# A two-layer hybrid decoder trunk: the third projection tile of layer 1 by token halves, and the norm's sums in column strips

## What is computed

```python
for l in range(DEPTH):                       # 2
    m = _mixer(_rmsnorm(h, norm_mix_pre[l]), ..., w_in[l], ..., w_out[l])
    h = h + _rmsnorm(m, norm_mix_post[l])
    f = _swiglu(_rmsnorm(h, norm_ffn_pre[l]), w_gate_up[l], w_down[l])
    h = h + _rmsnorm(f, norm_ffn_post[l])
# _rmsnorm(x, w) = x * rsqrt(mean(x * x) + EPS) * w
```

## Time and profile before

| | |
|---|---|
| Median of 3 runs | 1385.88 us (1385.72 to 1387.19) |
| The profiled execution | 1384.18 us, span 1382.4 us |
| Granted TensorE clock | 0.998 of 2.4 GHz |
| PE busy | 1362.3 us (99%) |
| VectorE busy | 1039.6 us (75%) |
| ScalarE busy | 634.8 us (46%) |
| GpSimd busy | 100.5 us (7%) |

### The profile page before, as it was taken

How to read it: one execution, slowest core, us unless ns; L and a number is a source line. 1 busy time by engine, 2 the same in 40 slices (tenths; PEclk the granted TensorE clock), 3 DMA queues, 4 the chain that set the end, 5 groups by cost and what they waited for, 6 DMA issues and landing times.

```text
span 1382.4 us, 29088 instructions
## 1 busy us (share of the span) xinstructions
PE 1362.3 (99%) x12172; PEld 1339.7 (97%) x12172; DVE 1039.6 (75%) x1675; ACT 634.8 (46%) x1230; POOL 100.5 (7%) x141
## 2 busy tenths in 40 slices
PE   8999999999999999999999999999999999999997
PEld 8999999999999999999989999999999999999996
DVE  7746796768999898754586458968789989886545
ACT  5235554557545455422442364545575445454221
POOL 0001221000000000011000012110000000000110
PEclk9999999999999999999999999999999999999999
DMA  6332243122333333355413313321232333333552
GB/s 210 107 107 78 67 116 105 45 69 81 103 108 114 101 101 108 115 174 183 130 62 108 111 60 99 107 94 36 79 92 93 120 95 112 104 106 121 176 178 93
DMA packets 67491, 147.46 MB, mean 107 GB/s; under 512 B 20128, under 2 KB 23584, under 8 KB 67360
## 3 DMA queue, kind: packets, MB, share of 16 engines
q1 hardware_dynamic: 59536, 119.90, 27.3%
q0 software_dynamic: 7824, 25.70, 5.5%
HBM read 132.79 MB, written 12.78 MB: 105 GB/s over the span
## 4 chain that ended last, share of the span: by engine, by line
PE 88%; DVE 8%; ACT 1%; issue 1%; DMA 1%; SPq 0%; DVEq 0%; ACTq 0%
PE PS L676 48%; PE PS L1231 8%; PE PS L1232 8%; PE PS L1233 8%; PE PS L682 5%; DVE Wl L1875 1%; DVE hT L1913 1%; DVE Xl L1892 1%; DVE mT L1912 1%; PE PS L870 1%; DVE conv L2002 1%; PE PS L1197 1%; PE PS L1016 1%; PE PS L842 1%; PE PS L854 1%
## 5 line engine op out<-in xcount | busy, mean ns | idle before, releaser
L1310 ACT ACTIVATE Wh<-stage 128x1024 fp32r<-128x1024 f32 x143 | 151.1, 1058 | 327.6 <-PE PS L676 299.5
L676 PE MATMUL PS<-Xh,Wh 128*128 128x260 f32 x1376 | 285.5, 289 | 2.9 <-DVE Xl L1934 2.2
L676 PE MATMUL PS<-Xh,Wl 128*128 128x260 f32 x1376 | 277.0, 283 | 0.0
L676 PE MATMUL PS<-Xl,Wh 128*128 128x260 f32 x1376 | 276.5, 282 | 0.0
L1875 DVE TENSOR_TENSOR Wl<-stage,Wh 128x1024 fp32r<-128x1024 f32 x143 | 174.6, 1222 | 105.7 <-ACT Wh L1310 105.0
L676 PEld LDWEIGHTS PS<-Xh,Wh 128*128 128x128 f32 x1376 | 211.4, 189 | 6.5 <-DVE Xl L1934 2.6
L676 PEld LDWEIGHTS PS<-Xh,Wl 128*128 128x128 f32 x1376 | 211.8, 188 | 0.0
L676 PEld LDWEIGHTS PS<-Xl,Wh 128*128 128x128 f32 x1376 | 211.7, 188 | 0.0
L1231 PE MATMUL PS<-XU,hiA 128*128 128x260 f32 x448 | 126.8, 283 | 0.0
L1231 PE MATMUL PS<-XU,hiB 128*128 128x260 f32 x448 | 126.8, 283 | 0.0
L1232 PE MATMUL PS<-XU,hiB 128*128 128x260 f32 x448 | 126.6, 283 | 0.0
(11 more groups left out here) (384 smaller groups left out, 2865.8 us busy)
## 6 DMA issues: line engine op xcount, KB each, us to landing
stage<-w_slabs SPq DMA_DIRECT2D x143, 512.0 KB, 3.3
raw<-w_slabs SPq DMA_DIRECT2D x136, 256.0 KB, 3.0
dst<-state_ret POOLq DMA_DIRECT2D x32, 256.0 KB, 3.8
dst<-state_gdn POOLq DMA_DIRECT2D x32, 256.0 KB, 3.8
out_gdn_sample<-dst POOLq DMA_DIRECT2D x16, 256.0 KB, 3.0
out_ret_sample<-dst POOLq DMA_DIRECT2D x16, 256.0 KB, 3.5
hT<-x_t SPq DMA_DIRECT2D x3, 520.0 KB, 6.5
out_y_t<-hT SPq DMA_DIRECT2D x3, 520.0 KB, 3.0
```

Of the source, the lines that this page charges most:

```text
L676: ins = mm(pj(slot)[:, a], w[:, ws, pos, :], x[:, a, :], start=first and w is Wh and x is xh, stop=last and w is Wl)
L1310: A(Wh[:, G % NW], stage[:, G % NS], ACT.Copy).then_inc(s["hi_split"], 1)
```

## The change

For layer 1's input projection (n = 0 of `first_halves`):

- PE: tile 2 is taken along in the second half: for each `k` its first half's three matmuls (`third(k, 0)`) are issued in the loop over half 1, and `third(k, 1)` after it. It lies in slot 3 (banks 6 and 7). The gate columns go to bank 4 and stand between the two.
- PE: the squares are summed otherwise. `strip_sums` sums four tiles by four matmuls, each 32 columns wide, into a strip of 32 partitions each; ScalarE copies the four strips to `part0` (`strips_copied`, scaled by 1/32), and `strips_added` adds them with one matmul by `ones`. Half 0: two strip groups and one `strips_added`, which is issued in half 1 at k = 4. Half 1: one group, one `strips_added`, and four sums one by one (`rest_sums`).
- ScalarE: squares go to `sqb0` and `sqb1` with eight places each and wait for no sum. `root_mean` of half 0 stands behind k = 5 of half 1 instead of k = 3. `hi(+2)` stands behind k = 4 of half 0.
- VectorE: `lo(+2)` stands ahead of `second_half_x` instead of behind it.

```diff
-        def slot_of(t):
-            return t if t < 3 else (t + 1) % 2
+        def slot_of(t, l=0):
+            return 3 if t == 2 and l else t if t < 3 else (t + 1) % 2
+        def gate_bank(l):
+            return 4 if l else 6
...
+            def strip_sums(l, n, a, k0, last):
+                pe.wait_ge(s["xsq_ready"], nth_square(l, n, k0 + 3, a))
+                for j in range(4):
+                    rows = rows_at(j, QB)
+                    ins = mm(PS[rows, 4 + a, 0:HC], ones[:, 0:QB], ((sqb0, sqb1)[a])[:, k0 + j, :], start=k0 == 0, stop=last, skip_group_check=True)
+                if last:
+                    ins.then_inc(s["x_sums"], KT - 1 if k0 else KT // 2)
+            def strips_added(l, n, a):
+                pe.wait_ge(s["xsq_ready"], part_at(l, n, a))
+                return mm(PS[:, 4 + a, 0:HC], ones, part0[:, a], start=True, stop=n == 2 or a == 0)
+            def rest_sums(l, k0, k1):
+                pe.wait_ge(s["xsq_ready"], nth_square(l, 0, k1 - 1, 1))
+                for k in range(k0, k1):
+                    mm(PS[:, 5, 0:HC], ones, sqb1[:, k, :], start=False, stop=k == KT - 1).then_inc(s["x_sums"], 1)
...
-                            if k and not (n and a):
+                            if n and a == 0 and k:
                                 add_sums(l, n, k - 1, a)
-                            if k == KT - 1 and not (n and a):
+                            if n and a == 0 and k == KT - 1:
                                 add_sums(l, n, k, a)
+                            if n == 0 and a == 0 and k == 5:
+                                strip_sums(l, n, 0, 0, False)
+                            if n == 0 and a and k == 4:
+                                strips_added(l, n, 0).then_inc(s["x_sums"], 1)
...
+                            if a and n == 0:
+                                third(k, 0)
+                            if a and n == 0 and k == 4:
+                                strip_sums(l, n, 1, 0, True)
+                            if a and n == 0 and k == KT - 1:
+                                strips_added(l, n, 1)
+                                rest_sums(l, 4, KT)
...
+                        if a == 0 and n == 0:
+                            strip_sums(l, n, 0, 4, True)
...
+                    else:
+                        gate_columns()
+                        for k in range(KT):
+                            third(k, 1)
...
+                if n == 0:
+                    A((sqb0, sqb1)[a][:, k], src, ACT.Square).then_inc(s["xsq_ready"], 1)
+                    return
...
+                def strips_copied(n, a, l):
+                    act.wait_ge(s["x_sums"], nth_norm(l, n) + (KT + KT // 2 if a else KT - 1))
+                    A(part0[:, a], PS[:, 4 + a, 0:HC], ACT.Copy, scale=1.0 / QB).then_inc(s["xsq_ready"], 1)
                 def second_x(n, l=l):
+                    if n == 0:
+                        act.wait_ge(s["tile_done"], l * TILES)
                     for k in range(KT):
                         round_x(n, k, 1, l)
+                        if k == (KT if n else 0):
+                            strips_copied(n, 0, l)
                         if k:
                             second_square(n, k - 1, l)
-                        if k == 3:
+                        if k == (3 if n else 5):
                             root_mean(n, 0, l)
+                        if n == 0 and k == SUM_AT:      # SUM_AT = 6
+                            strips_copied(0, 1, l)
...
                         square_x(0, k - 1, 0, l + 1)
+                        if k == 4:
+                            hi(G0 + SLABS + 2)
                         if k == 5:
                             root_mean(3, 1)
                     square_x(0, KT - 1, 0, l + 1)
-                    hi(G0 + SLABS + 2)
                     second_x(0, l + 1)
...
                 if l + 1 < DEPTH:
+                    lo(G0 + SLABS + 2)
                     second_half_x(3, l + 1)
-                    lo(G0 + SLABS + 2)
```

More of the change, by code:

```diff
@@ L269, in trunk @@
         assert (FT + 2) * HF <= ROWS and ROWS + 12 * P <= XU_N
+        sqb0 = at("sqb0", A0, ROWS, [P, KT, HC])
+        sqb1 = at("sqb1", A0, 0, [P, KT, HC])
+        part0 = at("part0", A0, KT * HC, [P, 2, HC])
+        assert ROWS + KT * HC <= XU_N
         PS = ctx.enter_context(nc.psum_tensor("PS", [P, 8, 512], fp32))
@@ L438, in trunk @@
         SPLIT = KT - 2 + 1
+        SUM_AT = 6
         def nth(l, n, k, a):
@@ L454, in nth_norm, with nth_square, part_at @@
             return (l * 2 + n // 2) * HN
+        def nth_square(l, n, k, a):
+            at = nth_norm(l, n) + 2 * (l if n else max(l - 1, 0))
+            if l == 0 and n == 0:
+                return at + 2 * (k + 1)
+            return at + a * KT + k + 1 + (0 if n else a + (a and k >= SUM_AT))
+        def part_at(l, n, a):
+            return nth_square(l, n, SUM_AT - 1 if a else KT - 1, a) + 1
         def wait_free(eng, G):
@@ L693, in add_sums @@
             def add_sums(l, n, k, a):
-                pe.wait_ge(s["xsq_ready"], nth_norm(l, n) + nth(l, n, k, a))
+                pe.wait_ge(s["xsq_ready"], nth_square(l, n, k, a))
                 mm(PS[:, 4 + a, 0:HC], ones, sqh[:, k % 2, a, :], start=k == 0, stop=k == KT - 1).then_inc(s["x_sums"], 1)
+            def strip_sums(l, n, a, k0, last):
[12 more added lines that the diff above has]
+                    mm(PS[:, 5, 0:HC], ones, sqb1[:, k, :], start=False, stop=k == KT - 1).then_inc(s["x_sums"], 1)
             def sum_added(l, n, a):
@@ L709, in second_sums @@
                 pe.wait_ge(s["second_added"], l + 1)
-                pe.wait_ge(s["xsq_ready"], nth_norm(l, 2) + HN)
+                pe.wait_ge(s["xsq_ready"], nth_square(l, 2, KT - 1, 1))
                 for k in (0, 1, KT - 2, KT - 1):
@@ L756, in third @@
                             wait_slab(l, n0 + 2)
-                            pe.wait_ge(s["o_ready"], (l + 1) * NC)
-                            pe.wait_ge(s["s_ready"], (l + 1) * NC)
+                            if n:
+                                pe.wait_ge(s["o_ready"], (l + 1) * NC)
+                                pe.wait_ge(s["s_ready"], (l + 1) * NC)
                         ins = mm3(3, a, (l * SLABS + n0 + 2) % NW, k, Xh[:, k], Xl[:, k], k == 0, k == KT - 1)
@@ L1017, in products, with gate_columns @@
                     ins.then_inc(s["kq_mm"], 1)
+                def gate_columns():
+                    pe.wait_ge(s["wba_ready"], l + 1)
+                    if l:
+                        pe.wait_ge(s["rb_ready"], l * 8 + 1)
+                    for j in range(0, KT, 2):
+                        for i in range(2):
+                            for a in range(2):
+                                rows = slice((2 * a + i) * BA_M, (2 * a + i + 1) * BA_M)
+                                ins = mm(PS[rows, gate_bank(l), 0:HC], wbs[:, j + i, :], hT[:, j + i, a, :], start=j == 0, stop=j == KT - 2, skip_group_check=True)
+                    ins.then_inc(s["ba_done"], 1)
                 if l == 0:
                     first_two()
+                    gate_columns()
                 else:
+                    at_step[0] += KT
                     first_halves(0, 0, 0)
[L1024 to L1031, removed]
+                proj(3 * KT if l == 0 else 2 * KT)
                 pe.wait_ge(s["badiag_ready"], l + 1)
@@ L1317, in square @@
                     h = 0 if a is None else a
-                    if n % 2 == 0:
+                    if n == 0:
+                        A((sqb0, sqb1)[a][:, k], src, ACT.Square).then_inc(s["xsq_ready"], 1)
+                        return
+                    if n == 2:
                         if k >= 2:
@@ L1923, in second_half_x @@
                     if n == 1:
-                        dve.wait_ge(s["xsq_ready"], nth_norm(l, 2) + KT + 4)
+                        dve.wait_ge(s["xsq_ready"], nth_square(l, 2, 3, 1))
                         step(V.tensor_tensor(sq2[:, 0:2], sq2[:, 0:2], sq2[:, 2:4], ALU.add))
-                        dve.wait_ge(s["xsq_ready"], nth_norm(l, 2) + KT + 6)
+                        dve.wait_ge(s["xsq_ready"], nth_square(l, 2, 5, 1))
                         V.tensor_tensor(sq2[:, 0:2], sq2[:, 0:2], sq2[:, 4:6], ALU.add).then_inc(s["second_added"], 1)
@@ L1962, in rope_tile @@
                     done(t)
-                    step.go(V.tensor_tensor(rsw[0:h2, u], PS[h2:P, banks(slot_of(t)), 0:HC], rope[0:h2, 1], ALU.mult))
-                    step.go(V.tensor_tensor(rsw[h2:P, u], PS[0:h2, banks(slot_of(t)), 0:HC], rope[h2:P, 1], ALU.mult))
-                    freed(V.tensor_tensor(rcs[:, u], pj(slot_of(t)), rope[:, 0], ALU.mult), t)
+                    step.go(V.tensor_tensor(rsw[0:h2, u], PS[h2:P, banks(slot_of(t, l)), 0:HC], rope[0:h2, 1], ALU.mult))
+                    step.go(V.tensor_tensor(rsw[h2:P, u], PS[0:h2, banks(slot_of(t, l)), 0:HC], rope[h2:P, 1], ALU.mult))
```

(15 more changed lines are left out.)

## The result

The changed kernel takes 1387.76 us (median of 16 runs), the kernel before 1385.78 (16 runs); the ratio is 1.002, 95% interval 1.0013 to 1.0027. The forecast was 1387.7. The medians differ by 2.0 us, the ratio is worth 2.8 (1.8 to 3.7), so the kernel is slower, by far less than 2%. The profiled execution has a span of 1385.6 us, 3.2 more than before.

A forecast was written before the change was run, and what follows sets the result against it. PE is busy 1362.3 of 1382.4 us, VectorE equally pacing layer 1's second half. PE ready for tile 3 0.7 us later, 1.0 waiting for slab +3, 0.1 restart: +1.8 on 1385.88 gives 1387.7 us, range 1385.0 to 1389.2.

The forecast's parts named there:

- The sums: Layer 1 norm sums on PE: strips overlap, 0.75 us a group; 4.9 us against 7.0, 2.1 less, little kept.
- the first rival: Strip group at k = 4 of the second half: strips do not overlap, 2.06 us a group, 1389.0 us; chance 0.12.
- The moved slab: VectorE and ScalarE between halves: splitting slab +2 first makes the second half's first tile 1.1 us late at PE.
- The second rival: Start of the second half: VectorE is not late and slab 3 is in time, -0.3 us, 1385.6 us; chance 0.2.
- The second half on PE: PE waits for tiles 1 and 3, then is slower at 1.09 us a step; ready for tile 3 0.7 us later.
- The fourth rival: Second half, steps 5 to 7: ScalarE's coupling to PE's sums paces them, 1 us or more, 1388.7 up; chance 0.08.
- What is late next: Norm factor 4.3 us late; PE waits 1.0 us for slab +3, tile 3 starts 1.8 later; tile 5 just holds.
- The sum: Whole kernel: 1.8 us more, 1385.88 + 1.8 = 1387.7 us.
- the forecast's "no change": Whole kernel: measurement can tell about 0.2%, 2.8 us, so the forecast +1.8 us would read as no change.

The follow-up runs named there:

- new sums alone: Kernel before with strip sums and eight places for squares, no third tile in the halves, slab +2 unmoved: ratio 0.9994 to before, tile 3 after 29.95 us.
- slab 3 early: Changed kernel with slab 3 of layer 1 rounded ahead of the root mean and split ahead of the rope table's second half: ratio 1.0004 to before.
- split twice: Changed kernel with slab +2 split twice on VectorE ahead of the second half: one run, tile 3 after 32.9 us.
- third tile alone: Kernel before with tile 2 by halves in the second half, slab +2 moved ahead and gate columns in bank 4, old sums kept: ratio 1.0003 to before.
- the filled kernels: idle time filled, and split twice with 22 thrown-away matmuls added between the halves: tile 3 after 31.5 and 32.8 us.
- idle time filled: Changed kernel with 13 thrown-away matmuls added between the halves where PE stands idle: ratio 1.0005 to before, tile 3 after 31.5 us.

## Why the prediction was right, point by point

- **The sums.** A group of strips cost 0.77 us against 0.75 taken from the gate columns. Strips overlap; the first rival falls. That little of the 2.1 us would be kept was right, and stronger than written: with strips alone less than 0.1 us of it reached tile 3.
- **The moved slab.** First tile of the second half 1.1 us late was forecast; 0.9 measured (the remainder started at 697.22, 0.18 of it the layer's later start; forecast was 697.2). The second rival (VectorE not late) falls; the doubled split shows that one more split goes to the end in full, 1.24 us.
- **The second half on PE.** There was a wait of 0.61 at the second tile (k = 1), as forecast. The one forecast at k = 3 did not come, since PE, slowed, was 1.2 us behind that tile. There was none for the tiles of k = 6 and 7: ScalarE waited 1.92 for the sum at k = 4, and its tile 7 (remainder from 707.59) was still in time. The fourth rival falls. But the step missed a term: the clock. I took PE's pace in this half as 0.12 us a matmul from end to end, and it was 0.22 for 3.0 us. On the path that is 1.1 us.
- **What is late next.** A wait of 1.0 us for slab 3 was forecast, 0.89 measured; moving the slab gave back 1.0. No gap at tile 5.
- **The sum.** +1.8 us was forecast for the stretch. Measured with the clock held it is 31.5 - 30.0 = 1.5, and as it runs 2.6. The other terms were 0.3 too high together (0.2 of it in VectorE's lateness), and the missing one is 1.1. By medians the whole kernel moved 2.0 us; by the ratio of the runs 0.2%, 2.8 us, on the very border that the forecast's "no change" was given for. That the median fell on 1387.7 is in part luck: the forecast lacked a whole term of 1.1 us, in a measurement whose single runs scatter by more than that. The mechanism was right but for this term.
- **Where the expected gain went.** The 2.1 us of matmuls taken away stood in waits: with the new sums alone PE's listed waits in the stretch grow from 1.3 to 3.2 us. In the changed kernel they are 4.6, 3.3 more than before, and its slow matmuls take 1.4 us more than at full clock (14 of them from 699.71 take 3.2 us, where the same with a start behind a wait take 1.8); 3.3 + 1.4 - 2.1 is the 2.6 us. Of the 1.4 us some 0.3 would otherwise have been a wait for the tile of k = 3, which leaves the 1.1 on the path. Of the wait of 1.68 ahead of the second half 0.9 is VectorE's lateness behind the split; the rest is PE being ready sooner, as the new sums alone show (10.4 against 11.2). The wait at slab 3 follows from the late last sum, and the clock from the idle time between the halves.

## What to carry to other kernels

At a border where PE runs as fast as another engine feeds it, taking matmuls away can gain nothing (here 2.1 us of work gave under 0.1), and one more instruction in the feeding engine's chain can be paid in full (here 1.24 us); look instead for PE work that needs only what is there already and put it into the wait (here five steps of a tile, worth 2.7 us). Ask of each result that comes later whether the next slab or buffer is queued behind its consumer, and take the slab out of that queue where the engine stands idle. New idle time on PE can cost more than its length, since the clock may fall behind it: look for the granted clock in windows of a few us, and ask who paces PE there (the same fall cost 1.1 us in one kernel here and 0.1 in another). Test a clock effect with matmuls whose result is thrown away.

## What the runs showed of the hardware

The granted clock fell to 0.50 (1.2 GHz) for about 3 us after PE had been idle for 1.68, busy for nine matmuls and idle for 0.61 us (changed; the same with slab 3 early), and after 2.94 us of idle time at once (split twice). It stayed at 1.00 with waits of 0.95 and 0.79 us (new sums alone), of 1.09 and 0.60 (third tile alone), and with the filled 1.7 us followed by 0.60. The Trainium skill (TensorE: Matmul & The Clock Gate, Part 1) says that the gate has two states, one of them half the rate, and goes by how busy the engine has been; the 0.50 and the filled kernels agree. I had not expected idle times of under 2 us to bring it about, and only one execution of each kernel was profiled, so how surely it falls from run to run stays open. The granted clock of a whole run is known for every run, to three digits: its mean is 0.9958 over the changed kernel's 16 runs and 0.9973 over 10 with the idle time filled, where one fall to half for 3 of 1386 us would make 0.001. This leans toward a fall in most runs but does not show it, since the kernels whose profile has no fall lie anywhere from 0.9965 to 0.9973 and slab 3 early, which has one, at 0.9964.

Four fp32 matmuls of 32 columns into four strips, 260 columns moved, take 0.77 us of PE's time between full-width matmuls (changed), where one full-width fp32 matmul takes 0.44 (709.96 to 710.40 in the same trace).
